# Feed forward: one level of Strassen's scheme in three quarters of each first matrix

## The reference

```python
def sq_relu_mlp(h, w1, w2):
    a = jax.nn.relu(h @ w1)
    return (a * a) @ w2

for i in range(DEPTH):                       # DEPTH = 2
    h = rms_norm(x, norm_mix[i])
    ...
    x = x + y
    h = rms_norm(x, norm_ffn[i])
    x = x + sq_relu_mlp(h, ffn_w1[i], ffn_w2[i])
```

## Time and profile before

| what | value |
|---|---|
| median of 3 runs | 2901.2 us (2900.65 to 2901.77) |
| the profiled execution's own time | 2900.2 us |
| span of its trace | 2898.4 us |
| busy share of PE, PE's weight loads, ACT, DVE, POOL | 99%, 82%, 56%, 38%, 14% |
| granted TensorE clock | 0.999 |
| mean traffic of the DMA engines | 172 GB/s |

### The profile page before, as it was taken

One profiled execution on the slowest core, in us unless ns is written; L12 is line 12 of the kernel. 1 busy time (PEld: TensorE's weight loads), 2 busy tenths in 40 slices (PEclk: granted clock), 3 DMA queues, 4 the chain that ended last, 5 costly groups with the idle time before them and its releaser, 6 DMA issues.

```text
span 2898.4 us, 35689 instructions
## 1 busy us (share of the span) xinstructions
PE 2870.2 (99%) x13354; PEld 2380.0 (82%) x13354; DVE 1091.8 (38%) x2229; ACT 1618.6 (56%) x2413; POOL 407.1 (14%) x472
## 2 busy tenths in 40 slices
PE   9999999999999999999999999999999999999999
PEld 7989889888887778888887887888877788788887
DVE  6554736211214654112126114423254611642235
ACT  7675767545445765445456545545455644655454
POOL 1111111111111001111110111111111011111110
PEclk9999999999999999999999999999999999999999
DMA  9776867788887328888885787887878488778884
GB/s 247 153 159 135 179 138 160 162 193 193 194 192 170 88 55 205 190 195 194 192 195 113 157 195 164 196 199 193 183 180 193 87 185 194 169 187 192 204 191 116
DMA packets 137005, 499.12 MB, mean 172 GB/s; under 512 B 15344, under 2 KB 15600, under 8 KB 136720
## 3 DMA queue, kind: packets, MB, share of 16 engines
q0 software_dynamic: 67296, 245.59, 47.8%
q1 hardware_dynamic: 68688, 249.59, 28.3%
q10 hardware_dynamic: 864, 1.78, 0.2%
HBM read 494.81 MB, written 2.10 MB: 171 GB/s over the span
## 4 chain that ended last, share of the span: by engine, by line
PE 95%; ACT 2%; DVE 2%; DVEq 1%; issue 0%; ACTq 0%
PE ps L1168 77%; PE ps L1187 5%; PE ps L1536 3%; PE ps L1287 1%; PE ps L1477 1%; PE ps L1456 1%; PE ps L1683 1%; ACT arena L1039 1%; PE ps L1390 1%; PE ps L1248 0%; PE ps L1270 0%; PE ps L1661 0%; PE ps L1466 0%; DVE XT L2260 0%; PE ps L1245 0%
## 5 line engine op out<-in xcount | busy, mean ns | idle before, releaser
L479 ACT ACTIVATE wh<-raw 128x1024 fp32r<-128x1024 f32 (+1 forms) x465 | 489.8, 1053 | 931.0 <-PE ps L1168 900.2
L1168 PE MATMUL ps<-HH,wh 128*128 128x512 f32 x2224 | 870.5, 391 | 2.9 <-DVE HL L2268 2.1
L1168 PE MATMUL ps<-HH,wl 128*128 128x512 f32 x2224 | 865.8, 389 | 0.0
L1168 PE MATMUL ps<-HL,wh 128*128 128x512 f32 x2224 | 865.6, 389 | 0.0
L463 POOL DMA_DIRECT2D wl<-weights x465 | 405.3, 872 | 2455.9 <-ACT wl L483 2455.9
L1168 PEld LDWEIGHTS ps<-HH,wh 128*128 128x128 f32 x2224 | 417.5, 188 | 94.1 <-issue 5.0
L1168 PEld LDWEIGHTS ps<-HL,wh 128*128 128x128 f32 x2224 | 417.5, 188 | 87.7 <-issue 1.4
L1168 PEld LDWEIGHTS ps<-HH,wl 128*128 128x128 f32 x2224 | 417.4, 188 | 87.3
L483 ACT ACTIVATE wl<-raw 128x1024 fp32r<-128x1024 f32 (+1 forms) x465 | 483.7, 1040 | 0.0
L1168 PE MATMUL ps<-MH,wh 128*128 128x512 f32 x1056 | 411.9, 390 | 0.7 <-DVE ML L2148 0.7
L1168 PE MATMUL ps<-MH,wl 128*128 128x512 f32 x1056 | 410.9, 389 | 0.0
(11 more groups left out here) (329 smaller groups left out, 3007.2 us busy)
## 6 DMA issues: line engine op xcount, KB each, us to landing
raw<-weights SPq DMA_DIRECT2D x468, 512.0 KB, 5.7
wl<-weights POOLq DMA_DIRECT2D x465, 512.0 KB, 7.8
XT<-x SPq DMA_DIRECT2D x4, 512.0 KB, 8.4
out<-XT SPq DMA_DIRECT2D x3, 512.0 KB, 2.7
arena<-tables POOLq DMA_DIRECT2D x1, 1024.0 KB, 11.0
arena<-table_h ACTq DMA_DIRECT2D x1, 640.0 KB, 5.7
arena<-swaps_a POOLq DMA_DIRECT2D x1, 576.0 KB, 8.2
out<-XT SPq DMA_DIRECT2D x2, 256.0 KB, 2.4
```

Of the source, the lines that this page charges most:

```text
L479: act_f(wh[:, n, 0:w], raw[:, n, 0:w], ACT.Copy)
L1168: op = mm(bank(g, t), w[:, slot, at:at + P], x[:, first + kt, :], start=(kt == 0 and w is wh and x is xh), stop=(kt == n_k - 1 and w is wl ...
```

## The change

In quarters 1 to 3 of each feed forward (the first stays as it was) the product with `w1` goes by one level of Strassen's scheme (in Winograd's form). The contraction is halved (even and odd tiles), the 1024 features of a quarter are taken as 4 sets of 256 (two blocks of 128), and the tokens as two blocks of 256. For a pair of contraction tiles, two blocks of features and two of tokens, eight block products of 256 columns (before: four matmuls of 512, times three) become seven, on sums of blocks, times three. A set (`twist_set`) takes two slabs and 4 pairs of contraction tiles: 4 x 7 x 3 = 84 matmuls of 256 columns into seven half banks of one group.

- **Sums of weights.** Of the four blocks in a twisted slab, three are used as they are (`given`); the fourth is only read in sums. DVE makes four sums of blocks for each set (`twist_raw`, 4 instructions), ACT their high parts (`twist_high`), DVE the low parts (`twist_low`). For a twisted slab ACT splits 768 columns in place of 1024, and POOL's adding DMA is 768 columns wide; the splitting waits for `twist_raw`.
- **Sums of the input.** In the first quarter DVE multiplies the input by gain and scale (`scaled_input`, 8 instructions, before the relus of the first set). After the first quarter's second set DVE makes four sums of blocks (`input_sums`) and all low parts, and ACT the high parts (`scaled_highs`, `sum_high`), into `HH`, `HL` and the new `SH`, `SL`. PE waits for them (`xs_done`) ahead of quarter 1.
- **Sums of the products.** After each set ACT copies one half bank (`twist_copy`, when the first of the seven is done), DVE adds in four instructions (`twist_sums`), ACT does the relu and two squares on 1024 columns (`twist_square`), DVE the low part (`twist_hidden`).
- In the second feed forward, four memsets of DVE move from before it to behind it, ahead of `h_ready`.

```diff
                 pool.wait_ge(w_hi, slab + 1)
-                pool.dma_start(wl[:, n, :], weights[slab], accum_op=ALU.add).then_inc(w_lo[n], 16)
+                first = 256 if slab in TWISTED else 0
...
-                act_f(wl[:, n, 0:w], raw[:, n, 0:w], ACT.Identity, scale=-1.0).then_inc(w_hi, 1)
+                at = 256 if twisted(s) else 0
+                if at:
+                    act.wait_ge(tw_raw, twist_of(s) + 1)
+                act_f(wl[:, n, at:w], raw[:, n, at:w], ACT.Identity, scale=-1.0).then_inc(w_hi, 1)
...
+            def twist_high(k):
+                act.wait_ge(tw_raw, k + 1)
+                act_f(t_hi[k % 2], t_raw, ACT.Copy).then_inc(tw_hi, 1)
...
+            def twist_copy(k, g):
+                act.wait_ge(tw_first, k + 1)
+                act_f(tw[:, 7], tw_bank(g, 0)[:, 0], ACT.Copy).then_inc(tw_copied, 1)
...
+            def twist_square(k, i, sp):
+                act.wait_ge(tw_sum, k + i + 1)
+                act_f(tw_out, tw_out, ACT.Relu)
+                act.drain()
+                act.wait_ge(split_done, sp.value(2 * i))
+                act_f(hf2, tw_out, ACT.Square)
+                act_f(MH[:, 2 * i:2 * i + 2, :], tw_out, ACT.Square).then_inc(split_hi, 2)
...
+            def scaled_highs(last_up, layer):
+                wait_used(act, last_up)
+                act.wait_ge(xs_ready, layer + 1)
+                act_f(HH[:, :, 0:256], XS[:, :, 0:256], ACT.Copy)
+                act_f(HH[:, 1:KT:2, 256:S], XS[:, 1:KT:2, 256:S], ACT.Copy).then_inc(xs_hi, 1)
...
-                    set_of(4)
-                    if q == 3:
+                    scaled_highs(s0 + 3, layer)
+                    high_parts(s0 + 12, 1)
+                    for n in range(4):
+                        sum_high(n, layer)
+                    high_parts(s0 + 13, 3)
...
+                def twist_quarter(q):
+                    s, k, sp = c.take("slab", 8), k0 + 4 * (q - 1), c.take("split", 8)
+                    g = c.take("group", TWIST_SETS)
+                    for i in range(TWIST_SETS):
+                        high_parts(s + (4 + 2 * i), 1)
+                        twist_copy(k + i, g + i)
+                        high_parts(s + (5 + 2 * i), 1)
+                        if i < 2:
+                            twist_high(k + 2 + i)
+                        twist_square(k, i, sp)
+                    high_parts(s + 12, 4)
...
+                    if q < 3:
+                        twist_high(k0 + 4 * q)
+                        c.take("group")
+                        s = c.take("slab", 4)
+                        high_parts(s + 4, 2)
+                        twist_high(k0 + 4 * q + 1)
+                        high_parts(s + 6, 2)
...
+            def twist_set(k):
...
+                g, s = c.take("group"), c.take("slab", 2)
+                wait_set_free(pe, g)
+                def product(at, left, right, opens, closes):
+                    x_hi, x_lo = right
+                    w_hi_lo = left
+                    for n, (w, x) in enumerate(((0, x_hi), (0, x_lo), (1, x_hi))):
+                        op = mm(tw_bank(g, at // 2)[:, at % 2, :], w_hi_lo[w], x, start=opens and n == 0,
+                                stop=closes and n == 2, skip_group_check=True)
+                    return op
...
+                for j in range(2):
+                    slot = (s + j).mod(SLOTS)
+                    wait_low(s + j)
+                    for p in range(2):
+                        n = 2 * j + p
+                        opens, closes = n == 0, n == 3
+                        def given(block):
+                            at = 256 * block + P * p
+                            return wh[:, slot, at:at + P], wl[:, slot, at:at + P]
+                        def made(m):
+                            return (t_hi[k % 2][:, m, j, P * p:P * p + P], t_lo[k % 2][:, m, j, P * p:P * p + P])
+                        def plain(t, odd):
+                            at = slice(256 * t, 256 * t + 256)
+                            return HH[:, 2 * n + odd, at], HL[:, 2 * n + odd, at]
+                        def summed_x(m):
+                            return (SH[:, m, n, :], SL[:, m, n, :])
+                        op = product(0, given(1), plain(0, 0), opens, closes)
+                        if closes:
+                            op.then_inc(tw_first, 1)
+                        product(2, given(2), plain(0, 1), opens, False)
+                        product(7, given(3), summed_x(2), opens, False)
+                        if n == 0:
+                            pe.wait_ge(tw_low, k + 1)
+                        product(6, made(3), plain(1, 1), False, closes)
+                        product(5, made(0), plain(1, 0), opens, False)
+                        product(3, made(2), summed_x(0), False, closes)
+                        op = product(4, made(1), summed_x(1), False, closes)
...
+            def ffn(layer):
                 s1 = c.take("split", KT)
                 for q in range(4):
                     s = c.take("split", 8)
-                    features(4, HH, HL, nothing if q else split_ready(s1), between=None if q else norm_sum, at=2)
                     if q == 0:
+                        features(4, HH, HL, split_ready(s1), between=norm_sum, at=2)
                         scale_read()
-                    features(4, HH, HL, nothing)
+                        features(4, HH, HL, nothing)
+                    else:
+                        if q == 1:
+                            pe.wait_ge(xs_done, 5 * layer + 5)
+                        for i in range(TWIST_SETS):
+                            twist_set(12 * layer + 4 * (q - 1) + i)
                     features(4, MH, ML, split_ready(s))
                     features(4, MH, ML, nothing)
...
+            def twist_raw(k, s):
+                n = s.mod(SLOTS)
+                for m in range(2):
+                    dve.wait_ge(w_load[n + m], s.div(SLOTS).times(16).value(16))
+                dve.drain()
+                b12, b11, b21, b22 = (raw[:, n:n + 2, 256 * m:256 * m + 256] for m in range(4))
+                v.tensor_tensor(t_raw[:, 0], b12, b11, ALU.subtract)
+                v.tensor_tensor(t_raw[:, 1], b22, b12, ALU.subtract)
+                dve.drain()
+                v.tensor_tensor(t_raw[:, 2], b22, t_raw[:, 0], ALU.subtract)
+                dve.drain()
+                v.tensor_tensor(t_raw[:, 3], b21, t_raw[:, 2], ALU.subtract).then_inc(tw_raw, 1)
...
+            def twist_low(k):
+                dve.wait_ge(tw_hi, k + 1)
+                v.tensor_tensor(t_lo[k % 2], t_raw, t_hi[k % 2], ALU.subtract).then_inc(tw_low, 1)
...
+            def twist_sums(k):
...
+                g, s = c.take("group"), c.take("slab", 2)
+                wait_used(dve, s + 1)
+                free = acc_free[g.mod(2)]
+                dve.wait_ge(tw_copied, k + 1)
+                v.tensor_tensor(tw[:, 0:5:4], tw[:, 7:8].broadcast_to((P, 2, 256)), tw_bank(g, 1), ALU.add)\
+                    .then_inc(free, 2)
+                dve.drain()
+                v.tensor_tensor(tw[:, 5:7], tw[:, 4:5].broadcast_to((P, 2, 256)), tw_bank(g, 2), ALU.add)
+                dve.drain()
+                v.tensor_tensor(tw[:, 1:3], tw[:, 5:7], tw_bank(g, 3), ALU.add).then_inc(free, 1)
+                v.tensor_tensor(tw[:, 3], tw[:, 5], tw_bank(g, 2)[:, 1], ALU.add).then_inc(free, 1)
+                dve.drain().then_inc(tw_sum, 1)
...
+            def twist_hidden(i, sp):
+                dve.wait_ge(split_hi, sp.value(2 * i + 2))
+                at = slice(2 * i, 2 * i + 2)
+                v.tensor_tensor(ML[:, at, :], hf2, MH[:, at, :], ALU.subtract).then_inc(split_done, 2)
...
+            def scaled_input(layer):
+                for t in range(KT):
+                    gain = par[:, P_FFN + 8 * layer + t:P_FFN + 8 * layer + t + 1]
+                    v.scalar_tensor_tensor(out=XS[:, t, :], in0=XT[:, t, :], scalar=gain, in1=rsn,
+                                           op0=ALU.mult, op1=ALU.mult)
+                dve.drain().then_inc(xs_ready, 1)
...
+                s1, s2, s3, s4 = x_sum
+                v.tensor_tensor(s1, x21, x22, ALU.add).then_inc(xs_sum, 1)
+                dve.drain()
+                v.tensor_tensor(s2, s1, x11, ALU.subtract).then_inc(xs_sum, 1)
+                v.tensor_tensor(s3, x11, x21, ALU.subtract).then_inc(xs_sum, 1)
+                dve.drain()
+                v.tensor_tensor(s4, x12, s2, ALU.subtract).then_inc(xs_sum, 1)
...
+                def twist_quarter(q):
+                    k, sp = k0 + 4 * (q - 1), c.take("split", 8)
+                    s = c.at["slab"]
+                    dve.sem_inc(split_src, 8)
+                    for i in range(TWIST_SETS):
+                        twist_sums(k + i)
+                        if i == 0:
+                            twist_low(k + 2)
+                            twist_raw(k + 3, s + 6)
+                        if i == 1:
+                            twist_low(k + 3)
```

(64 more changed lines are left out.)

74 lines of the change are left out of this document (57 added, 17 removed).

## The result

The changed kernel takes **2875.61 us** (median of 4 runs, 2874.51 to 2876.13); the kernel before took 2900.93 beside it (4 runs, 2900.26 to 2901.77). The ratio is 0.9912, with a 95% interval of 0.9899 to 0.9924, so 25.3 us less.

A forecast was written before the change was run, and what follows sets the result against it. PE's matmul stream was taken as the bound: 261.2 us removed, 241.5 added, stalls 0, so -19.7; 2900.2 less 19.7 is 2880.5, and the median 1.0 above gives 2881.5 us. Forecast range 2879.5 to 2883.5, wider range to 2890.

The forecast's parts named there:

- 2016 x 0.1198 = 241.5 us: PE's added stream in six quarters: 2016 matmuls of 256 columns at 0.1198 us each, against 261.2 us removed.
- both rows are of the very form: Reason for taking 0.1198 us: two earlier streams of 256 columns, at 0.1198 and 0.1200, were held to match the new sets.
- The lower bound, 0.1134: New matmuls at half of 0.2267 us, no fixed part: 228.6 us, a gain of 32.6, total 2868.6; chance 0.02.
- The weight loads: Loads before PE's new matmuls: taken to overlap; the skill's page gave 0.213 us a matmul, 430 us, a loss of 169.
- Slab 13 of the first quarter: ACT starts it at 613.5, after added copies; landing 623.7, PE at it 624.79: room 1.1 us, or late by 0.9.
- the eight scalings: DVE ahead of the second feed forward's first relus: 5.4 us, sliding ACT's slab by 3.8; room 0.6, or late by 1.4.
- I take 0: Stalls of PE on slabs: 0 at median landing, up to 0.9 + 1.4 at the longest, up to 8 with slow raw sums.
- late slabs now and then: Rival: late slabs in first quarters and first sets give back 2 to 9 us, 2883.5 to 2890.5; chance 0.20.
- after two more sets: When PE wants the slab issued behind a quarter's first-set raw sums: at 20.1 us, room 2.3 us (0.3 at longest landing).
- the third set: Sign of being wrong: PE waiting for the first slab of a quarter's third set, because of the adding DMA.
- No change: Rival: adding DMA landings near 10.9 us in every set eat the gain, 2895.4 to 2907; chance 0.05.
- both slower rivals: Weight loads set PE's pace at 0.188 us a matmul, 3019, chance 0.02; adding DMA paces every set, 2927, chance 0.05.

The follow-up runs named there:

- e4: The kernel before, with the six quarters' `w1` matmuls cut into two of 256 columns, same products, no sums: 2915.31 us, ratio 1.0043.
- e2: The changed kernel with 64 bytes of padding ahead of `arena`, which then starts on a multiple of 128 bytes: 2878.25 us, ratio 0.9915.
- e3: The changed kernel with 64 bytes of padding ahead of every buffer: 2875.16 us, ratio 0.9904.
- e1: The changed kernel with products on sums of weights first in each round of 21 matmuls: 2875.46 us (one run).
- e13: The kernel before with `w1` matmuls of the six quarters cut to 256 columns, and `wh`, `wl` 64 bytes off: 2957.99 us, ratio 1.0202.
- e12: The changed kernel with the raw sums of weights made three times in the first set of each twisted quarter: 2893.4 us, ratio 0.9978.
- e14: The changed kernel with all new products' operands 64 bytes apart (scaled input in `HH_64`, `HL_64`, `HL` 128 bytes later): 2887.75 us, ratio 0.9954.
- e6: The changed kernel with `wh`, `wl` and `arena` 64 bytes off a multiple of 128: 2936.9 us, ratio 1.0117.
- e7: The changed kernel with `HL`, `ML`, `wh`, `arena` 64 bytes off a multiple of 128 and the others on one: 2925.35 us, ratio 1.0078.
- e5: The changed kernel with 64 bytes of padding ahead of `raw`, so `wh`, `wl` are 64 off and `arena` at 0: 2934.61 us, ratio 1.0111.

## Why the prediction was right in kind and wrong in size

- **The bound and the mechanism: right.** PE's stream sets the time, there is no gap in the chain of the changed quarters, and the gain is the difference of two streams.
- **The term that failed** is "2016 x 0.1198 = 241.5 us". It was sized too large: it measured 2016 x 0.11745 = 236.8, so 4.7 less: with it the sum gives 2881.5 - 4.7 = 2876.8, and the rest, 1.2 us, is within the spread of executions. The sentence that failed with it is "both rows are of the very form". They were of the form in columns (e4 confirms 0.1198 there), but in the earlier trace rows both operands start on the same remainder, and in 15 of a round's 21 matmuls one operand or both lie in `arena`, 64 off. Putting `arena` on the same remainder took back 3.2 of the 4.7 us (e2, by the chain), shifting everything took back nothing (e3), the distances followed the operands through a change of order (e1), and e13 showed on one and the same matmul that placement alone moves its distance. So where the buffers start to each other is shown as the cause of some two thirds of the 4.7 us. The other 1.5 us, why matmuls among sums keep less than 0.12 in e2, and by what rule placement acts, stay open.
- **The bounds.** The lower bound, 0.1134, was taken as "no fixed part" and given 2 in 100; that was the only chance for anything below 2879.5. The measured 2875.61 lies between that range and the 2868.6 of the bound. e13 reached 0.1134, in a kernel whose 512 columns cost more; no placement of the changed kernel did. Having named the bound, the range should have come further down towards it.
- **The weight loads** did not set the pace: loads of 187 ns stand beside matmuls 117 ns apart, so loads overlap each other and the matmuls. The rule of the Trainium skill weighed in the prediction (page "TensorE: Matmul & The Clock Gate", section "The mechanism") led to an estimate of 0.213 us a matmul; this trace disagrees with it.
- **The hidden work: right.** The first set ran as walked, to 0.3 us, DVE busy for 8.51 of the 9.87 us behind it (forecast near 90%). Slab 13 of the first quarter started on ACT at 612.80 (forecast 613.5), the eight scalings took 5.39 us (forecast 5.4), and "I take 0" for the stalls held in all three places. The rival *late slabs now and then* did not come; e12 shows that it was a real one, since 5.66 us more of DVE in one set of each quarter gives back 17.8 of the 25.3 us. Its waits stand at a quarter's fourth set, where the prediction's own count ("after two more sets") leads; the third set, named among the signs of being wrong, was a slip. *No change* and both slower rivals are gone with the empty list of waits.
- **The adding DMA** got lighter, and the share of 0.81 in a twisted quarter's product with `w1` is the number forecast, but partly by luck. The forecast took every adding DMA there at 384 KB; in that window they were of both sizes (KB each, median us to landing):

```profile
wl<-weights POOLq DMA_DIRECT2D x5, 384.0 KB, 6.0
wl<-weights POOLq DMA_DIRECT2D x3, 512.0 KB, 7.3
```

The next quarter's product has 0.82, the whole feed forward 0.86 where it was 0.89.

## What to carry to other kernels

Price a stream by its own distance between starts, times the number of matmuls, and take that distance from a row that shares the new stream's operands and where they start, not its shape alone; where no such row exists, let the range reach the full columns' rate. Halving the columns is not free (15 us here), so a scheme with fewer products has to pay for its smaller shape first. A room of some 3.5 us was enough here in all six quarters, and 2.86 us more work in it cost nothing; repeat the tightest piece two and three times to learn how far it is from showing.

## What the runs showed of the hardware that was not expected

- The distance of float32 matmuls with a weight load each depends on where the buffers start in a partition, relative to each other. With all on the same remainder by 128 bytes it was 0.2269 us for 512 columns and 0.1200 for 256; with the weights 64 bytes off, 0.2333 and 0.1134. For three matmuls (a high by high, high by low, low by high) that is 681 and 360 ns against 700 and 340, 20 ns a triple up and down, at a granted clock of 2.4 GHz. What makes the difference was not found; e14 shows that more than the remainder by 128 goes into it, and e6, e7 and e14 that it isn't settled by the two operands of each matmul alone.
- 16 unused columns ahead of `raw`, which shift it and all buffers behind it by 64 bytes, moved the whole kernel by 59 us (e5), more than twice what Strassen's scheme gave. No placement that was tried beats that of the changed kernel; e3 (2875.16) is the same within the spread.
